# Conditioning rows in buffers of their own beside a ring of weight units

## The reference

```python
def adaln(cond, w_ada, b_ada):
    return jnp.split(jax.nn.silu(cond) @ w_ada + b_ada, ADA_CHUNKS, axis=-1)

m_lat = adaln(c, w_ada, b_ada)        # 6 chunks of 2048
m_ctx = adaln(c_ctx, w_ada, b_ada)    # the first two chunks are used
h = h * (1 + scale) + shift
```

## Time and profile before

| what | before |
|---|---|
| runs, median of 3 (lowest to highest) | 2975.66 us (2967.76 to 2975.87) |
| profiled execution, span | 2968.8 us |
| TensorE matmul busy, weight loads busy | 2862.9 us (96%), 2612.1 us (88%) |
| VectorE, ScalarE, GpSimd busy | 1887.0, 1594.9, 795.8 us |
| DMA | 610.66 MB, mean 206 GB/s |

### The profile page before, as it was taken

One profiled execution on the slowest core, in us unless ns is written; L12 is line 12 of the kernel. 1 busy time (PEld: TensorE's weight loads), 2 busy tenths in 40 slices (PEclk: granted clock), 3 DMA queues, 4 the chain that ended last, 5 costly groups with the idle time before them and its releaser, 6 DMA issues.

```text
span 2968.8 us, 54565 instructions
## 1 busy us (share of the span) xinstructions
PE 2862.9 (96%) x19302; PEld 2612.1 (88%) x19302; DVE 1887.0 (64%) x2292; ACT 1594.9 (54%) x2364; POOL 795.8 (27%) x650
## 2 busy tenths in 40 slices
PE   8999899999999999999999999989989999999999
PEld 8988899998899988888888888889988888888888
DVE  5666777866677876533355666766776765555554
ACT  5555566555577765332344666665656654344443
POOL 3464234303344421111102421244424530000000
PEclk9999999999999999999999999999999999999999
DMA  7864577657777776344456554576767875555554
GB/s 278 268 227 139 201 245 240 207 180 237 245 242 250 244 236 194 100 141 148 158 164 186 192 167 154 193 245 231 245 218 244 271 256 184 185 190 184 187 188 163
DMA packets 174590, 610.66 MB, mean 206 GB/s; under 512 B 19344, under 2 KB 27664, under 8 KB 174096
## 3 DMA queue, kind: packets, MB, share of 16 engines
q1 hardware_dynamic: 162432, 591.47, 60.3%
q10 hardware_dynamic: 10720, 12.51, 1.4%
q0 software_dynamic: 1328, 5.24, 0.5%
HBM read 598.66 MB, written 5.77 MB: 204 GB/s over the span
## 4 chain that ended last, share of the span: by engine, by line
PE 69%; DVE 12%; ACT 8%; DMA 6%; issue 5%; DVEq 0%; ACTq 0%; SPq 0%
PE acc L1653 21%; PE acc L1657 19%; PE acc L1655 8%; PE acc L1656 8%; DVE wlo L1073 5%; ACT whi L615 4%; DMA raw<-w_ada 2%; ACT cond_products L611 2%; DMA raw<-w_up 1%; PE acc L1641 1%; DVE conv_out L1167 1%; PE acc L1643 1%; PE acc L1644 1%; PE acc L1651 1%; PE sums L1875 1%
## 5 line engine op out<-in xcount | busy, mean ns | idle before, releaser
L1073 DVE TENSOR_TENSOR wlo<-raw,whi 128x1024 fp32r<-128x1024 f32 x864 | 1139.0, 1328 | 852.4 <-ACT whi L615 851.0
L1657 PE MATMUL acc<-operand,wlo 128*128 128x256 f32 (+1 forms) x4816 | 1397.4, 290 | 0.0
L615 ACT ACTIVATE whi<-raw 128x1024 fp32r<-128x1024 f32 x864 | 908.1, 1056 | 902.0 <-PE acc L1657 513.6
L1655 PE MATMUL acc<-operand,whi 128*128 128x256 f32 (+1 forms) x3136 | 936.9, 299 | 64.5 <-DVE wlo L1073 43.4
L1657 PEld LDWEIGHTS acc<-operand,wlo 128*128 128x128 f32 x4816 | 923.1, 192 | 14.3
L1656 PE MATMUL acc<-operand,whi 128*128 128x256 f32 (+1 forms) x3136 | 925.5, 295 | 0.0
L1655 PEld LDWEIGHTS acc<-operand,whi 128*128 128x128 f32 x3136 | 604.6, 193 | 90.2 <-DVE wlo L1073 47.5
L1656 PEld LDWEIGHTS acc<-operand,whi 128*128 128x128 f32 x3136 | 605.3, 193 | 12.5
L1653 PE MATMUL acc<-operand,whi 128*128 128x512 f32 x1680 | 600.6, 400 | 8.0 <-DVE operand L1417 5.9
L475 POOL TENSOR_TENSOR cond_products<-cond_products 128x512 f32<-128x512 f32 x192 | 255.4, 1330 | 1270.2 <-ACT cond_products L611 1269.6
L1653 PE MATMUL acc<-ffn_act,whi 128*128 128x512 f32 x1344 | 473.0, 396 | 3.6 <-DVE wlo L1073 3.6
(11 more groups left out here) (220 smaller groups left out, 2481.4 us busy)
## 6 DMA issues: line engine op xcount, KB each, us to landing
raw<-w_ada SPq DMA_DIRECT2D x256, 512.0 KB, 4.3
raw<-w_in SPq DMA_DIRECT2D x224, 512.0 KB, 3.9
raw<-w_up SPq DMA_DIRECT2D x176, 512.0 KB, 4.3
raw<-w_down SPq DMA_DIRECT2D x88, 512.0 KB, 4.4
raw<-w_fg SPq DMA_DIRECT2D x88, 512.0 KB, 4.1
raw<-w_fu SPq DMA_DIRECT2D x88, 512.0 KB, 3.9
raw<-w_fd SPq DMA_DIRECT2D x88, 512.0 KB, 3.3
raw<-w_o SPq DMA_DIRECT2D x32, 512.0 KB, 4.5
```

Of the source, the lines that this page charges most:

```text
L615: act.activation(whi[j % RING][:], raw[j % RING][:], ACT.Copy).then_inc(hi_done, 2 if st.entries[j % st.upb - 1] == (None, ADA_VEC) else 1)
L1073: dve.tensor_tensor(wlo[j % RING][:], raw[j % RING][:], whi[j % RING][:].bitcast(F32), ALU.subtract).then_inc(lo_done, 2 if prev[0] is Non ...
L1655: pe.matmul(out_, h[:, x, f], mov[:, 0], start=first, stop=False)
L1657: ins = pe.matmul(out_, l[:, x, f], mov[:, 0], start=False, stop=last)
```

## The change

- The ring holds weight units alone; a body has 8 entries instead of 12. The step numbers inside bodies (for example 10 to 6, 11 to 7) are moved so that they stand at about the same weight unit.
- An item is loaded as eight halves of two tiles, 256 KB each: six into three buffers `cond_rows`, scaled in place by ScalarE, one half behind each of the first six `hi` of a body; two into two buffers `cond_vec_rows`, summed by VectorE behind the `lo` of steps 1 and 4.
- GpSimd adds the six halves 512 wide into `cond_pair`, then adds its two rows (256 wide), then VectorE's row (256 wide): seven adds instead of nine.
- SP loads the halves at fixed places among the weight loads (`SP_FIRST`, `SP_REST`), the last three in the next body's loads where bodies have eight units; it waits for `ada_ops` or `cond_vec`.
- The matrix is laid out in HBM in the order of the items, with the context's 16 items ahead of the tokens' 48 and two rows of padding.
- The scratch of GpSimd's software queue shrinks to 4096 bytes, and the tiles begin at byte 4224.
- More stages run as loops to their last body (`joined`).

```diff
+COND_SLOTS, VEC_SLOTS = 3, 2
+COND_HALVES = 6
+COND_OPS = 7
+VEC_OPS = 4
+VEC_AT = (1, 4)
+SP_FIRST = {4: ("v0",), 5: ("v1", 0), 6: (1,), 7: (2,)}
+SP_REST = {9: 3, 10: 4, 11: 5}
...
-            if ada and j in ADA_AFTER:
-                self.cond.append(len(self.entries))
-                self.entries.append((None, ADA_AFTER.index(j)))
         self.upb = len(self.entries)
+        self.rest_later = bool(ada) and self.upb <= min(SP_REST)
...
+            def cond_load(n, h):
+                sp.wait_ge(ada_ops, n * COND_OPS + (3, 4, 5, 8, 8, 9)[h])
+                sp.dma_start(cond[h % COND_SLOTS][:], half_of(n, h)).then_inc(cond_in[h % COND_SLOTS], 16)
+            def vec_load(n, i):
+                sp.wait_ge(cond_vec, n * VEC_OPS + 2 * i + 2)
+                sp.dma_start(crow[i][:], half_of(n, COND_HALVES + i)).then_inc(crow_in[i], 16)
...
+                    sp.wait_ge(lo_done, unit(st, b, j) + 1)
...
+                    if rest and j + 8 in SP_REST:
+                        cond_load(b + (st.ib - 1), SP_REST[j + 8])
+                    if st.ada and j in SP_FIRST:
+                        for what in SP_FIRST[j]:
...
+                for h in range(1, COND_HALVES):
+                    pool.wait_ge(cond_made, n * COND_HALVES + (h + 1))
+                    if h == 1:
                         pool.wait_ge(ada_red, n + 1)
+                        pool.tensor_tensor(CP[:], cond[0][:], cond[1][:], ALU.add).then_inc(ada_ops, 1)
                     else:
+                        pool.wait_ge(ada_ops, done + (h - 1))
+                        pool.tensor_tensor(CP[:], CP[:], cond[h % COND_SLOTS][:], ALU.add).then_inc(ada_ops, 1)
...
+                pool.wait_ge(ada_ops, done + 5)
+                pool.tensor_tensor(CA, CA, CP[:, 1, :], ALU.add).then_inc(ada_ops, 1)
+                pool.wait_ge(cond_vec, n * VEC_OPS + 2 * VEC_OPS)
+                pool.wait_ge(ada_ops, done + 6)
+                pool.tensor_tensor(CA, CA, CV[:], ALU.add).then_inc(ada_ops, 1)
...
+            def hi(st, b, j):
                 act.wait_ge(raw_in[j % RING], filled(st, b, j))
+                act.wait_ge(used, unit(st, b, j) + 1)
+                act.activation(whi[j % RING][:], raw[j % RING][:], ACT.Copy).then_inc(hi_done, 1)
+            def condition(st, b, h):
+                n = b + st.ib
+                rows = cond[h % COND_SLOTS]
+                act.wait_ge(cond_in[h % COND_SLOTS], n * 32 + (h // COND_SLOTS + 1) * 16)
+                for x in range(2):
+                    ins = act.activation(rows[:, x, :], rows[:, x, :], ACT.Copy, scale=cond_silu(st, h, x))
+                ins.then_inc(cond_made, 1)
...
+                    if st.ada and j - RING < COND_HALVES:
+                        condition(st, b, j - RING)
...
+                    if st.ada and j - RING in VEC_AT:
+                        condition(st, b, VEC_AT.index(j - RING))
...
-                pe.wait_ge(ada_ops, n * ADA_OPS + (ADA_OPS + 1))
+                pe.wait_ge(ada_ops, n * COND_OPS + 2 * COND_OPS)
...
-    nc = bacc.Bacc("TRN2", target_bir_lowering=False, num_devices=1)
+    nc = bacc.Bacc("TRN2", target_bir_lowering=False, num_devices=1, dynamic_dma_scratch_size=4096)
```

More of the change, by code:

```diff
@@ L122, in number @@
         n += st.ada * st.bodies
-    for st, after in zip(stages, stages[1:] + [None]):
-        st.next = after
+    for st, prior, after in zip(stages, [None] + stages[:-1], stages[1:] + [None]):
+        st.prior, st.next = prior, after
     assert n == ADA_ITEMS
@@ L174, in build @@
     with ExitStack() as ctx:
-        place = {"at": 16512}
+        place = {"at": 4224}
         def here(n_bytes):
@@ L238, in build @@
         astep = sem("astep")
+        cond_in = [sem(f"cond_in{i}") for i in range(COND_SLOTS)]
+        crow_in = [sem(f"cond_vec_in{i}") for i in range(VEC_SLOTS)]
+        cond_made = sem("cond_made")
+        cond_vec = sem("cond_vec")
         ada_ops = sem("ada_ops")
-        ada_sum = sem("ada_sum")
         ada_red = sem("ada_red")
@@ L308, in grouped, with cond_silu @@
             return unit(st, b, st.last[gb]) + 1 + RING
-        def cond_silu(st, u, x):
-            k = (KT if st.ib >= ADA_CTX else 0) + UK * u + x
+        def cond_silu(st, half, x):
+            k = (KT if st.ib >= ADA_CTX else 0) + 2 * half + x
             return CS[:, k:k + 1]
         def joined(st):
-            return st.next is not None and bool(st.next.ada) == bool(st.ada) and (
-                (st.next.ib >= ADA_CTX) == (st.ib >= ADA_CTX) or not st.ada)
+            return st.next is not None and st.kind not in SUMMED
         def groups_before(st):
@@ L437, in load @@
                         first_rows(3)
-            mark = lambda entries: [e[0] is None for e in entries]
-            prior = [(0, 0)] * RING
-            for st in stages:
-                own = st.entries[-RING:]
-                first = mark(prior) != mark(own)
-                if first:
-                    load(st, 0, prior)
-                if st.bodies > int(first):
-                    with sp.Fori(int(first), st.bodies) as b:
-                        load(st, b, own)
-                prior = own
+                    if rest and j + 8 in SP_REST:
+                        cond_load(b + (st.ib - 1), SP_REST[j + 8])
+                    if st.ada and j in SP_FIRST:
+                        for what in SP_FIRST[j]:
+                            if what in ("v0", "v1"):
+                                vec_load(b + st.ib, int(what[1]))
+                            else:
+                                cond_load(b + st.ib, what)
+                    if st.ada and not st.rest_later and j in SP_REST:
+                        cond_load(b + st.ib, SP_REST[j])
+            for st in stages:
+                owed = st.prior is not None and st.prior.rest_later
+                peel = owed != st.rest_later
+                if peel:
+                    load(st, 0, owed)
+                if st.bodies > int(peel):
+                    with sp.Fori(int(peel), st.bodies) as b:
+                        load(st, b, st.rest_later)
             for n, (k0, k1) in enumerate(((0, 8), (8, 12), (12, 14), (14, KT))):
@@ L594, in _ @@
         def _(act):
-            def hi(st, b, j, before=(0, 0), item=None):
-                gb, u = st.entries[j % st.upb]
-                if gb is None and u == ADA_VEC:
-                    return
+            def hi(st, b, j):
                 act.wait_ge(raw_in[j % RING], filled(st, b, j))
-                if before[0] is not None:
-                    act.wait_ge(used, unit(st, b, j) + 1)
-                elif before[1] != ADA_VEC:
-                    act.wait_ge(ada_ops, item * ADA_OPS + (ADA_ADDS[before[1]] + 1))
-                else:
-                    act.wait_ge(used, unit(st, b, j) + (1 - RING))
-                if gb is None:
-                    for x in range(UK):
-                        ins = act.activation(prod[j % RING][:, x, :], raw[j % RING][:, x, :], ACT.Copy,
-                                             scale=cond_silu(st, u, x))
-                    ins.then_inc(hi_done, 1)
-                    return
-                act.activation(whi[j % RING][:], raw[j % RING][:], ACT.Copy).then_inc(
-                    hi_done, 2 if st.entries[j % st.upb - 1] == (None, ADA_VEC) else 1)
+                act.wait_ge(used, unit(st, b, j) + 1)
[7 more added lines that the diff above has]
+                ins.then_inc(cond_made, 1)
             def post(st, b, gb):
@@ L1036, in _ @@
             body(st_bb, 0)
-            body(st_bb, 1, then={0: lambda: merged_hi(0), 2: lambda: merged_hi(1), 8: lambda: merged_hi(2)})
+            body(st_bb, 1, then={0: lambda: merged_hi(0), 2: lambda: merged_hi(1), 5: lambda: merged_hi(2)})
             merged_hi(3)
@@ L1548, in _ @@
                 for j in range(RING, RING + st_g.upb):
-                    second = st_g.entries[j - RING][0] is not None and AT_B <= s + 1 < AT_B + NB_
+                    second = AT_B <= s + 1 < AT_B + NB_
                     if second:
@@ L1583, in _ @@
             body(st_bb, 0)
-            body(st_bb, 1, then={1: lambda: merged_lo(0), 3: lambda: merged_lo(1), 9: lambda: merged_lo(2)})
+            body(st_bb, 1, then={1: lambda: merged_lo(0), 3: lambda: merged_lo(1), 6: lambda: merged_lo(2)})
             merged_lo(3)
```

141 lines of the change are left out of this document (55 added, 86 removed).

## The result

The changed kernel takes 3035.93 us (median of 4 runs, 3033.54 to 3041.93), the kernel before beside it 2972.62. The ratio is 1.0214, 95% interval 1.0201 to 1.0228: slower by 2.1%, where 2946 us and a gain were forecast, and above the range's end of 2992.

What follows compares the result with a forecast made beforehand. TensorE was taken as the bound, losing time to late operand splits. Terms of -52, -5 and +27 made -30 us, taken off the median 2975.66 for 2946 us; range 2910 to 2992 for 8 in 10.

Steps and rivals of the forecast that it cites:

- Removed: units in the ring: Weight loads on TensorE: waits for the split's `wlo` nearly vanish without conditioning units in the ring; 52 us gained.
- the forecast 24.2 us: Sign of being right: up2 bodies, from one closing reduction to the next, fall from 25.9 to 24.2 us.
- branch_a (-5): In branch_a, TensorE's 9.1 us of waits for the evacuation at three body ends shrink; 5 us gained, bounds 0 and 9.
- branch_a's end hides it behind the evacuation: At branch_a's body ends the later conditioning sum costs nothing, being covered by the evacuation.
- Transfers (0): Loads of the halves: half 3 up to 0.7 us late but hidden, half 5 just in time; counted 0.
- Added: a later end of the item (+27): At body ends TensorE waits for GpSimd's last add, 0.5 or 0.9 us in 41 bodies; 27 us lost.
- the closing wait eats more than the ring gives: Rival: at body ends the wait for the sum is 2.0 us a body, giving 3001 us; chance 0.15.
- GpSimd keeps up: GpSimd's seven adds per item take about 9 us of each 23.5, so it keeps pace.
- attention 0: Gates stage's attention part: reordered conditioning work between softmax steps counts 0, with bounds of 6 us either way.

Runs made afterwards that it cites:

- e5: Changed kernel with the closing reduction behind the next body's second unit in most stages, and ScalarE's last three halves one step later: 2953.07 us, 0.9936 of the kernel before.
- e6: e5 with halves 0 and 1 loaded one weight unit sooner and VectorE's two halves later: 2951.89 us, 0.9929 of the kernel before.
- e10: Changed kernel with GpSimd's last two adds of each item 32 columns wide instead of 256 (sums incomplete): 2977.49 us, 1.0016 of the kernel before.
- e2: Changed kernel with eight useless matmuls ahead of the closing wait in 45 bodies: 3023.57 us, 1.0172 of the kernel before.
- e9: Kernel before, with only GpSimd's last add of each item held until TensorE used the body's last unit: 3057.71 us, 1.0277 of the kernel before.
- e1: Changed kernel with each item's closing reduction moved behind the next body's first unit, except at three stage ends: 2972.74 us, 0.9988 of the kernel before.
- e7: Changed kernel with ScalarE's last three halves one step later, the reduction still at the body's end: 3194.09 us, 1.0743 of the kernel before.
- e8: e6 with the closing reduction three units into the next body instead of two: 2951.64 us, 0.9923 of the kernel before.

## Why the prediction was wrong, by its own steps

**Removed: units in the ring (-52).** Right. 58.2 us of waits for `wlo` became 6.9, so -51, and none of the changed kernel's variants has more than 11 us of them. In up2 the 20.1 us are gone entirely; the weight loads of the window above wait for the sum alone, and for 0.2 us more:

```profile
PEld ada_sums L1675 <- issue: 19.5, 9, 4.2
```

Its bodies come near the forecast 24.2 us only where the closing wait is gone: 23.9 to 24.9 in e5, mostly 24.85 in e6. The body of the changed kernel that ends at 930.92 took 27.87. The 24.2 doesn't quite follow from the prediction's own terms either: 23.48 and a wait of 0.9 make 24.4.

**branch_a (-5).** Wrong by about 4. The evacuation's wait of 9.1 us went, but the closing reductions of the stage's four bodies (at 2006.83, 2034.49, 2061.34 and 2086.92) wait 3.79, 1.60, 1.60 and 1.80 us, 8.8 together. "branch_a's end hides it behind the evacuation" failed: the cover was the very wait that the same change removed.

**Transfers (0).** This failed first. The prediction saw half 3 up to 0.7 us late and said that 5 us behind it hid that, and called half 5 "just in time". ScalarE waited 173.1 us in 153 places. In the body of w_in shown above the waits are 0.4 to 0.8 us at halves 3, 4 and 5, through SP's order (a freed slot's load stood 2.4 us behind a weight load) and a landing of 4.5 us for an assumed 4. The fault is that half 5 isn't hidden: it stands at the head of the chain to the sum, and the next step had already used up that chain's slack. The range's worst landing, 0.7 us late, was kept for a rival only.

**Added: a later end of the item (+27).** The mechanism and its place were right, its size was not: 85.6 us, 1.9 in each of 46 bodies, for 0.5 and 0.9 in 41. The adds were taken well (means 1.23 and 1.10 us, one slow and one quick together). No closing wait stands behind kv, down1 and down2, as forecast, and one of 2.1 us behind the gates stage. What failed is the start of the chain, 0.95 us behind the release, where 1.9 stood in a body of w_in and some 4.6 in one of up2 (with a half in time e10's item would be ready after 3.4 + 0.72 + 0.55 + two gaps of 0.08 = 4.8 us, under the 5.48, and 44 us of waits are left there). It is the rival "the closing wait eats more than the ring gives", given 0.15, with the price it named, 2.0 us a body; that alone would have made 3001 us.

**The clock (no term).** The other half of the miss. No step asked what TensorE does after a wait. The missing clock grew by 42.9 us. The windows show 1.2 GHz behind two of the waits (and full speed behind a third), e2 takes the clock back by filling the wait, and e9 loses it by the wait alone. The idle time alone, with the wait at its real size, grew by 23.0 us, and the span by 62.9.

**GpSimd keeps up; attention 0.** Right, within its bounds: GpSimd is busy 693.0 us, and the gates stage grew by 2.8 us from its first to its last weight load, with the closing wait of 2.1 us behind it.

## What to carry to other kernels

When work leaves a shared buffer for one of its own, look at where its result is taken. The sum was ready 5.5 us early; its new place in the body used up all of that, so in the body of w_in shown a half that came 0.9 us late made TensorE's wait 0.9 us longer. Take such a result a unit or two into the next body, where most of its lateness is hidden (14.9 us of closing waits in e1 for 85.6), and put a step that needs a buffer back behind the time that the buffer's load really takes.

Price a bare wait of TensorE that returns every 25 us at more than its length. Each us of closing wait came with 0.4 to 0.6 us of missing clock on the average (34.2 for 96.2 in e9, 42.9 for 85.6 in the change, 122.9 for 197.4 in e7), though single waits cost 1.7 us of clock or none. It is a rough price: e5 and e8 too miss 9 to 12 us more clock than the kernel before, with 16.2 and 6.0 us of closing waits, and where that goes wasn't looked for.

## What the runs showed of the hardware

- Behind a wait of 1.70 us TensorE lost as much again to the lower clock level, behind one of 1.29 us nothing. The prediction had no such cost; the kernel before was granted 0.993.
- VectorE slows beside GpSimd as well. Its `cond_vec_sum` step has two SBUF inputs and takes 0.48 us, but when it starts beside a wide add it takes 1.6; both rows come from the changed kernel (two steps in the first, 0.48 + 1.60):

```profile
923.84 2.11 DVE L1077 SCALAR_TENSOR_TENSOR cond_vec_sum<-cond_vec_rows,cond_silu,cond_vec_sum 128x256 f32<-128x256 f32 x2
...
924.37 1.30 POOL L497 TENSOR_TENSOR cond_pair<-cond_pair,cond_rows 128x512 f32<-128x512 f32 x1 [2.19 <-ACT cond_rows L623]
```

  The group's mean is 0.78 us, 0.49 before. Of the 192 steps in this trace 55 took over 1.3 us, and each of them ran beside an add of GpSimd. By the Trainium skill (GPSIMD Engine Reference, Specifications) the two engines share SBUF interfaces and contend in just this case; the rows agree, and show that VectorE pays too. The step ahead of it, with one SBUF input (L1079, L1068 before), also went from a median of 0.35 us to 1.39; two cases were looked at, both beside a wide add.
- A GpSimd add of 32 columns takes 0.55 to 0.72 us in the mean, one of 256 1.10 to 1.23.
- Halving a load hastened it little or not: the 256 KB halves landed in 4.5 us (`cond_rows`) and 3.9 us (`cond_vec_rows`) in the median, 512 KB of the same matrix in 4.3 before. A half has as many packets as a whole: SP's queue moved 162432 packets in 1128 loads and stores before and 199296 in 1384 after, 144 each time.
